# Seven half-size products in place of eight in one feed-forward of a transformer kernel on Trainium2

## The reference

```python
D_MODEL, SEQ, D_FF, FFN_HALF = 1024, 512, 2816, 0.5

def swiglu(h, w13, w2):
    gate, up = jnp.split(h @ w13, 2, axis=-1)
    return (jax.nn.silu(gate) * up) @ w2

# in second_block, layer 0
x = x + jnp.concatenate([y_mix, y_mem], axis=-1) @ w_out[layer]
x = x + FFN_HALF * swiglu(rms_norm(x, norm_g[layer, 2]), ffn_w13[layer, 1], ffn_w2[layer, 1])
```

## Time and profile before

| | |
|---|---|
| median of 3 runs | 2980.66 us (2978.97 to 2982.44) |
| span of the profiled execution | 2978.9 us |
| PE busy | 99%, 13494 matmuls |
| PEld busy | 81% |
| DVE, ACT, POOL busy | 60%, 32%, 8% |
| DMA | 287.55 MB, mean 97 GB/s |

### The profile page before, as it was taken

One profiled execution on the slowest core, in us unless ns is written; L12 is line 12 of the kernel. 1 busy time (PEld: TensorE's weight loads), 2 busy tenths in 40 slices (PEclk: granted clock), 3 DMA queues, 4 the chain that ended last, 5 costly groups with the idle time before them and its releaser, 6 DMA issues.

```text
span 2978.9 us, 36307 instructions
## 1 busy us (share of the span) xinstructions
PE 2962.1 (99%) x13494; PEld 2414.2 (81%) x13494; DVE 1802.2 (60%) x2379; ACT 956.6 (32%) x1292; POOL 224.5 (8%) x105
## 2 busy tenths in 40 slices
PE   9999999999999999999999999999999999999999
PEld 7888788788888888888887888888888886688887
DVE  8897565667766555544467655556555567755542
ACT  4743632333222222222233322222222245332221
POOL 0044330000000000000032000002000021000000
PEclk9999999999999999999999999999999999999999
DMA  4222123223222222223332222232222231122233
GB/s 142 99 92 90 67 92 120 71 96 110 99 94 96 99 95 97 95 95 106 106 121 78 96 99 92 98 106 99 99 99 99 99 113 65 37 98 98 92 106 106
DMA packets 79304, 287.55 MB, mean 97 GB/s; under 512 B 8992, under 2 KB 9248, under 8 KB 78816
## 3 DMA queue, kind: packets, MB, share of 16 engines
q1 hardware_dynamic: 77904, 280.06, 27.9%
q0 software_dynamic: 1296, 6.03, 0.6%
HBM read 283.96 MB, written 2.10 MB: 96 GB/s over the span
## 4 chain that ended last, share of the span: by engine, by line
PE 97%; DVE 2%; ACT 1%; DMA 0%; issue 0%; POOL 0%; SPq 0%; POOLq 0%; ACTq 0%; DVEq 0%
PE ps L667 30%; PE ps L669 30%; PE ps L668 30%; PE ps L1056 1%; PE ps L1292 0%; PE ps L1255 0%; PE ps L831 0%; PE ps L820 0%; PE ps L744 0%; PE ps L1045 0%; PE ps L1258 0%; DVE w_lo L1906 0%; PE ps L806 0%; PE ps L839 0%; PE ps L951 0%
## 5 line engine op out<-in xcount | busy, mean ns | idle before, releaser
L667 PE MATMUL ps<-h_hi,w_hi 128*128 128x512 f32 (+1 forms) x2371 | 928.8, 392 | 3.0 <-DVE w_lo L1906 2.6
L669 PE MATMUL ps<-h_hi,w_lo 128*128 128x512 f32 (+1 forms) x2371 | 919.9, 388 | 0.0
L668 PE MATMUL ps<-h_lo,w_hi 128*128 128x512 f32 (+1 forms) x2371 | 919.6, 388 | 0.0
L1359 ACT ACTIVATE w_hi<-raw 128x1024 fp32r<-128x1024 f32 x524 | 554.0, 1057 | 1008.6 <-DMA raw<-in_wstream 1008.4
L1906 DVE TENSOR_TENSOR w_lo<-raw,w_hi 128x1024 fp32r<-128x1024 f32 x436 | 528.4, 1219 | 134.5 <-ACT w_hi L1359 123.6
L667 PEld LDWEIGHTS ps<-h_hi,w_hi 128*128 128x128 f32 x2371 | 445.6, 188 | 102.5 <-issue 7.7
L668 PEld LDWEIGHTS ps<-h_lo,w_hi 128*128 128x128 f32 x2371 | 445.6, 188 | 92.8 <-issue 3.1
L669 PEld LDWEIGHTS ps<-h_hi,w_lo 128*128 128x128 f32 x2371 | 445.3, 188 | 91.9
L667 PE MATMUL ps<-mid_hi,w_hi 128*128 128x512 f32 x1200 | 468.1, 390 | 0.0
L669 PE MATMUL ps<-mid_hi,w_lo 128*128 128x512 f32 x1200 | 466.9, 389 | 0.0
L668 PE MATMUL ps<-mid_lo,w_hi 128*128 128x512 f32 x1200 | 466.9, 389 | 0.0
(11 more groups left out here) (432 smaller groups left out, 2542.3 us busy)
## 6 DMA issues: line engine op xcount, KB each, us to landing
raw<-in_wstream SPq DMA_DIRECT2D x525, 512.0 KB, 3.2
x<-in_x SPq DMA_DIRECT2D x4, 512.0 KB, 6.3
x_in<-in_x POOLq DMA_DIRECT2D x8, 256.0 KB, 3.0
mem_x<-in_mem POOLq DMA_DIRECT2D x2, 1024.0 KB, 5.3
out<-x SPq DMA_DIRECT2D x8, 256.0 KB, 4.6
tmp<-in_ret_decay POOLq DMA_DIRECT2D x1, 1024.0 KB, 7.4
rope_r<-in_rope_r POOLq DMA_DIRECT2D x1, 512.0 KB, 4.0
mats<-in_mats SPq DMA_DIRECT2D x1, 256.0 KB, 7.9
```

Source lines behind the costliest of these rows:

```text
L667: nc.tensor.matmul(dst, hi_w, hi_x, start=first, stop=False)
L668: nc.tensor.matmul(dst, hi_w, lo_x, start=False, stop=False)
L669: return nc.tensor.matmul(dst, lo_w, hi_x, start=False, stop=last)
L1359: nc.scalar.activation(w_hi[:, n % HL], raw[:, r], ACT.Copy).then_inc(hi_ready, 1)
```

## The change

The product of `s0b_in` is computed in a form of Strassen's scheme (seven products instead of eight, with the sums of Winograd's form). The 1024 channels of x are cut in two halves, its 512 tokens in two halves, and the columns of a unit in gate and up: a 2 x 2 by 2 x 2 block product. A unit is one gate tile and one up tile of 128 columns; there are 22. Each of its seven products has 4 channel tiles x 3 matmuls of 256 columns.

- Weights come from a new tensor `pairs`: 22 units of 128 x 2048 (1 MB), as four blocks of 512 columns: gate and up of the first channel half, gate and up of the second, in the order that the slices of `unit_load` show. The stage `s0b_in` leaves the stream of panels. SP loads two blocks as they are and five more blocks, four of which a DMA then turns into sums: POOL issues `t1 += block`, `t2 += t1`, `t3 += block`, `t4 += t2`, each an accumulating DMA of 256 KB. The loaded block and the sums have two buffers (even and odd units); each load waits for the product of two units before that used the buffer.
- ACT makes the high parts in four slots of `w_hi` that all units share, so each waits for the same product of the unit before. DVE makes the low parts.
- The four sums of blocks of x are made once, by DVE, while `wo0` ends. `wo0` now runs its output tiles in the order 0, 4, 1, 5, ... (`PAIRED`), so that both channel halves of a pair are there. x takes its gain on ACT, squares are made by ACT and added by DVE.
- PE orders the products p1, p2, p4 of the unit before, p5, p6, p3, p7. p1, p6, p7 and p4 add up in one bank, and ACT or DVE takes each state out in between.
- The product of gate and up is kept unsplit; ACT and DVE split the 22 tiles at the end of the units and during the first output tile. The up side isn't multiplied by `rstd` any more; the output of `s0b_out` is (`rooted`).

SP's loads and POOL's sums:

```diff
+            def unit_load(u, i=None):
+                p = u % 2
+                src = A["pairs"][u] if i is None else A["pairs"][bass.ds(i * 2 + u, 1)].rearrange("a p n -> (a p) n")
+                later = i is not None
+                if later:
+                    sp.wait_ge(p2_done, at(u - 1, i, 2))
+                sp.dma_start((pairs_b if p else pairs_a)[:, 0:2], src[:, 0:2 * S].rearrange("p (a n) -> p a n", n=S)).then_inc(b_loaded[p], 16)
+                if later:
+                    sp.wait_ge(p5_done, at(u - 1, i, 2))
+                sp.dma_start(unit_raw("t1", p), src[:, 0:S]).then_inc(t1_loaded[p], 16)
+                if later:
+                    sp.wait_ge(p6_done, at(u - 1, i, 2))
+                sp.dma_start(unit_raw("t2", p), src[:, 3 * S:4 * S]).then_inc(t2_loaded[p], 16)
+                if later:
+                    sp.wait_ge(p3_done, at(u - 1, i, 2))
+                sp.dma_start(unit_raw("c", p), src[:, 3 * S:4 * S]).then_inc(c_loaded[p], 16)
+                if later:
+                    sp.wait_ge(p7_done, at(u - 1, i, 2))
+                sp.dma_start(unit_raw("t3", p), src[:, 2 * S:3 * S]).then_inc(t3_loaded[p], 16)
+                if later:
+                    sp.wait_ge(p4_done, at(u - 1, i, 2))
+                sp.dma_start(unit_raw("t4", p), src[:, S:2 * S]).then_inc(t4_loaded[p], 16)
...
+            unit_load(0)
+            loads(ST["mem0"].n + 4, ST["conv"].n + 3)
+            unit_load(1)
+            loads(ST["conv"].n + 3, ST["s0b_out"].n)
+            with sp.Fori(0, (UNITS - 2) // 2) as i:
+                for u in (2, 3):
+                    unit_load(u, i)
...
+            def unit_sums(u):
+                p = u % 2
+                src = A["pairs"][u]
+                pool.wait_ge(t1_loaded[p], 16 * (u // 2 + 1))
+                pool.dma_start(unit_raw("t1", p), src[:, 2 * S:3 * S], accum_op=ALU.add).then_inc(t1_summed[p], 16)
+                pool.wait_ge(t2_loaded[p], 16 * (u // 2 + 1))
+                pool.wait_ge(t1_summed[p], 16 * (u // 2 + 1))
+                pool.dma_start(unit_raw("t2", p), unit_raw("t1", p), accum_op=ALU.add).then_inc(t2_summed[p], 16)
+                pool.wait_ge(t3_loaded[p], 16 * (u // 2 + 1))
+                pool.dma_start(unit_raw("t3", p), src[:, 3 * S:4 * S], accum_op=ALU.add).then_inc(t3_summed[p], 16)
+                pool.wait_ge(t4_loaded[p], 16 * (u // 2 + 1))
+                pool.wait_ge(t2_summed[p], 16 * (u // 2 + 1))
+                pool.dma_start(unit_raw("t4", p), unit_raw("t2", p), accum_op=ALU.add).then_inc(t4_summed[p], 16)
+            for u in range(UNITS):
+                unit_sums(u)
```

PE's products and their order:

```diff
+            def half_products(kind, x, u, which, first, ks=range(KH)):
+                hi, lo, tile, col0 = X_OF[x]
+                dst, cols = unit_bank(u % 2, which), slice(col0, col0 + H)
+                for k in ks:
+                    sl = slice(P * k, P * k + P)
+                    w1, w0 = unit_high(kind)[:, sl], unit_low(kind, u % 2)[:, sl]
+                    x1, x0 = hi[:, tile + k, cols], lo[:, tile + k, cols]
+                    start = first and k == 0
+                    nc.tensor.matmul(dst, w1, x1, start=start, stop=False, skip_group_check=not first)
+                    nc.tensor.matmul(dst, w1, x0, start=False, stop=False, skip_group_check=not first)
+                    mm = nc.tensor.matmul(dst, w0, x1, start=False, stop=k == KH - 1, skip_group_check=not first)
+                return mm
+            Z1, Z2, Z3 = range(3)
+            def fourth(u, i=None):
+                pe.wait_ge(t4_low, at(u + 1, i, 2))
+                pe.wait_ge(c22_taken, at(u + 1, i, 2))
+                half_products("t4", "a22", u, Z1, False).then_inc(p4_done, 1)
+            def from_sixth(u, i=None, middle=None):
+                pe.wait_ge(t2_low, at(u + 1, i, 2))
+                pe.wait_ge(p1_copied, at(u + 1, i, 2))
+                half_products("t2", "s2", u, Z1, False).then_inc(p6_done, 1)
+                if middle:
+                    middle()
+                pe.wait_ge(c_low, at(u + 1, i, 2))
+                pe.wait_ge(c11_taken, at(u + 1, i, 2))
+                half_products("c", "v4", u, Z3, True).then_inc(p3_done, 1)
+                pe.wait_ge(t3_low, at(u + 1, i, 2))
+                pe.wait_ge(e_taken, at(u + 1, i, 2))
+                half_products("t3", "s3", u, Z1, False).then_inc(p7_done, 1)
+            def unit(u, i=None):
+                pe.wait_ge(b_low, at(u + 1, i, 2))
+                if u >= 2:
+                    pe.wait_ge(c21_taken, at(u - 1, i, 2))
+                else:
+                    pe.wait_ge(drained, ST["wo0"].t + DT)
+                half_products("b11", "a11", u, Z1, True).then_inc(p1_done, 1)
+                if u >= 2:
+                    pe.wait_ge(c12_taken, at(u - 1, i, 2))
+                half_products("b21", "a12", u, Z3, True).then_inc(p2_done, 1)
+                fourth(u - 1, i)
+                pe.wait_ge(t1_low, at(u + 1, i, 2))
+                half_products("t1", "r1", u, Z2, True).then_inc(p5_done, 1)
+                from_sixth(u, i)
+            def first_unit():
+                t = ST["wo0"].t
+                pe.wait_ge(b_low, 1)
+                pe.wait_ge(drained, t + KH + 1)
+                pe.wait_ge(x_low, 4 * KH - 3)
+                half_products("b11", "a11", 0, Z1, True).then_inc(p1_done, 1)
+                pe.wait_ge(drained, t + KH + 2)
+                pe.wait_ge(x_low, 4 * KH - 6)
+                half_products("b21", "a12", 0, Z3, True, range(KH - 1))
+                pe.wait_ge(t1_low, 1)
+                pe.wait_ge(drained, t + KH + 3)
+                pe.wait_ge(x_low, 4 * KH - 5)
+                half_products("t1", "r1", 0, Z2, True, range(KH - 1))
+                pe.wait_ge(x_low, 4 * KH - 2)
+                half_products("b21", "a12", 0, Z3, True, (KH - 1,)).then_inc(p2_done, 1)
+                pe.wait_ge(x_low, 4 * KH - 1)
+                half_products("t1", "r1", 0, Z2, True, (KH - 1,)).then_inc(p5_done, 1)
+                pe.wait_ge(x_low, 4 * KH)
+                from_sixth(0, middle=late_sum)
+            first_unit()
+            unit(1)
+            with pe.Fori(0, 8) as i:
+                for u in (2, 3):
+                    unit(u, i)
+            for u in range(18, UNITS):
+                unit(u)
+            pe.wait_ge(c21_taken, UNITS - 1)
+            gemm("s0b_out", gated_hi, gated_lo, (mid_split, lambda k: k + 1), F2, between=(KH, lambda: fourth(UNITS - 1)))
```

ACT's order of a unit (each `high_` waits for its sum or load and for the product of the unit before):

```diff
+            def high_t1(u, i=None):
+                act.wait_ge(t1_summed[u % 2], at(16 * (u // 2 + 1), i, 16))
+                if u:
+                    act.wait_ge(p5_done, at(u, i, 2))
+                half_high("t1", t1_high, u)
...
+            def unit(u, i=None):
+                high_t3(u, i)
+                first_copied(u, i)
+                high_b(u + 1, i)
+                if u == 1:
+                    act.wait_ge(p4_done, 1)
+                    nc.scalar.activation(tmp[:, 0, right], unit_bank(0, 0), ACT.Copy).then_inc(c21_taken, 1)
+                high_t4(u, i)
+                unit_gate(u - 1, i)
+                fifth_copied(u, i)
+                high_t1(u + 1, i)
+                high_t2(u + 1, i)
+                high_c(u + 1, i)
```

DVE's sums of x, the low parts and the order of a unit:

```diff
+            def low_t1(u, i=None):
+                dve.wait_ge(t2_summed[u % 2], at(16 * (u // 2 + 1), i, 16))
+                half_low("t1", t1_high, t1_low, u, i)
+            def low_t2(u, i=None):
+                dve.wait_ge(t4_summed[u % 2], at(16 * (u // 2 + 1), i, 16))
+                half_low("t2", t2_high, t2_low, u, i)
...
+            def halved_sums(q):
+                k = q // 2
+                dve.wait_ge(z_made, q + 1)
+                if q % 2 == 0:
+                    v.tensor_tensor(tmp[:, 0, right], tmp[:, 0, left], tmp[:, 0, right], ALU.subtract).then_inc(sums_made, 1)
+                    return
+                done(v.scalar_tensor_tensor(out=tmp[:, 2, right], in0=tmp[:, 0, right], scalar=-1.0, in1=tmp[:, 1, right],
+                                            op0=ALU.mult, op1=ALU.subtract))
+                v.tensor_tensor(tmp[:, 2, left], tmp[:, 2, right], tmp[:, 0, left], ALU.add).then_inc(sums_made, 1)
+                v.tensor_tensor(tmp[:, 3, left], tmp[:, 2, right], tmp[:, 1, left], ALU.add).then_inc(sums_made, 1)
...
+            def between_right(u, i=None):
+                p = u % 2
+                dve.wait_ge(p5_copied, at(u + 1, i, 2))
+                dve.wait_ge(p6_done, at(u + 1, i, 2))
+                v.tensor_tensor(stage[:, p, left], stage[:, p, right], unit_bank(p, 0), ALU.subtract).then_inc(e_taken, 1)
+            def second_right(u, i=None):
+                p = u % 2
+                dve.wait_ge(p7_done, at(u + 1, i, 2))
+                v.tensor_tensor(stage[:, p, right], stage[:, p, right], unit_bank(p, 0), ALU.subtract).then_inc(c22_taken, 1)
...
+            def unit(u, i=None):
+                second_right(u - 1, i)
```

(19 more changed lines are left out.)

389 lines of the change are left out of this document (374 added, 15 removed), and 2 rows, old and new, of the table STAGES.

## The result

| | us | |
|---|---|---|
| before | 2981.51 | median of 4 runs, 2978.97 to 2982.44 |
| after | 3075.73 | median of 4 runs, 3068.55 to 3080.16 |
| after / before | 1.032 | 95% interval 1.0307 to 1.0332 |
| predicted | 2988.0 | range 2965 to 3018 |

The change costs 94 us, 3.2%. Slower was the likeliest side, but by 7 us, and the time lies outside the range. The page shows the new thing at once: DMAs have 7% of the chain, where they had 0% before.

The account below looks back on a forecast made before the run. TensorE, busy 99%, was taken to bound the kernel. Stage terms -17.8 + 2.0 + 3.2 + 0.5 + 0.5 = -11.6 us, plus 19 for the DMA loop, gave +7.4 on the median 2980.66: 2988 us, range 2965 to 3018.

Parts of the forecast that it names:

- TensorE's part: In the rewritten stage, 256-column matmuls at 0.1199 us make a unit 10.07 us instead of 10.88: 17.8 us less.
- The mechanism: TensorE idles once per unit, about 0.9 us, until VectorE's subtraction of the seventh product, VectorE held by the fourth sum's DMA.
- The end: In the chain into the next stage, the eighth output tile's extra multiplication costs 0.5 us (0 to 0.7).
- loop one: Closed loop through VectorE's queue, from one fourth product to the next: 6.8 + L, 11.0 us per unit, +19 over 20 units.
- L: Time for one accumulating DMA of 256 KB to land: taken as 4.2 us, ends 3.0 and 5.3.
- loop two: Closed loop on GpSimd's queue, two sums waited for in a row: 2L + 0.58 + 0.54, 10.07 us at L = 4.5.
- The bandwidth estimate: A unit reads 3.93 MB with every add read twice: 9.9 to 10.4 us at the saturated stretches' rates.
- the saturation rival: DMA engines saturate in the new stage: 12.2 us per unit or L above 5, +41 to +43, 3011 us; chance 0.13.
- The rival's sign: In the changed profile, loads landing in 4 us too would show saturation.
- The start: At the stage's start, TensorE waits for the last output-projection tile's sums and splits: 2.0 us (0 to 4).
- My sign for a wrong account of it: A first wait over 5 us in the changed profile would mean the account of the start or engines is wrong.
- the reciprocal: In unit 1, the norm's reciprocal, 3.35 us on VectorE, delays the seventh product's bank: 3.2 us of wait (1 to 5).

Follow-up runs that it names:

- e2_no_adds: The changed kernel without the four accumulating DMAs of every unit, products taken with the blocks as loaded: 2975.98 us, ratio 0.9985 to the kernel before.
- e1_order: The changed kernel with VectorE's subtraction for the fourth product moved ahead of the next unit's lows of t2 and c: 3031.45 us.
- e9_three_sums: e1_order without the sum of t3, whose block is used as loaded: 3032.67 us.
- e7_pool_start: e4_pool_adds with ScalarE's and VectorE's queues reordered at the end of the output projection wo0: 2983.24 us.
- e8_mixed: e1_order's VectorE order and e11_start's start, with t1 and t3 summed by DMA, t2 and t4 by GpSimd's arithmetic: 2976.07 us.
- e11_start: The changed kernel with only ScalarE's and VectorE's queues reordered at the end of wo0, as in e7_pool_start: 3064.25 us.
- e3_copies: The changed kernel with the four accumulating DMAs of a unit made plain copies of the same size, same queue and waits: 3030.92 us.
- e4_pool_adds: The changed kernel with the four sums of a unit made by GpSimd's own arithmetic in place of DMAs: 2991.58 us.
- e6_filled: The changed kernel with 24 more matmuls of 256 columns per unit ahead of the fourth product's wait: 3081.61 us.

## Why the prediction was wrong

**What held.** TensorE's part: 0.12 us per matmul, a unit 10.07 forecast and 10.08 measured where nothing waits. The mechanism: TensorE waits once per unit, for the subtraction of the seventh product, with VectorE held by the fourth sum's DMA. The Trainium skill, Collectives: The Full Stack, section The bandwidth ceiling, says of the reducing step of a ReduceScatter that it is slower because the add needs two source reads, with a measured ratio of 1.93; the trace agrees in size, with a factor of 2.05 in packet time. The end: the step ahead of the next stage's first matmul is 0.93 us too long, 0.21 before, so 0.7 for the forecast 0.5, the upper end of its bounds. The Trainium skill, TensorE: Matmul & The Clock Gate, section Back-to-back issue gap, gives N/2.4 + 2.5 ns for an isolated matmul, by which I estimate 109 ns; the changed kernel's own steps are 120 again.

**The step that failed** is loop one's sum, "6.8 + L" with L = 4.2. The loop was the right one; three of its four terms were too small. Measured on the first unit of the round above, and on average over the 18 units:

| link | forecast | one unit | average |
|---|---|---|---|
| load of t4, to the issue of its sum | 3.1 | 4.6 | 4.7 |
| sum of t4, L | 4.2 | 4.6 | 6.2 |
| two lows, subtraction, to the matmul | 2.1 | 1.8 | 1.8 |
| fourth product, to the load's issue | 1.6 | 3.1 | 2.5 |
| together | 11.0 | 14.0 | 15.2 |

L is the largest part of the miss: 4.6 to 8.9 us, in 9 of 18 units over my upper bound of 5.3. I had added 0.2 us to it for the DMA share, and nothing to the load, while loads of 256 KB land in 3.3 to 3.7 us without the sums (e2_no_adds) and in 4.4 to 6.0 with them (medians by tile). And in 11 units the fourth product runs at the lower clock level, mostly behind a long wait that the loop itself makes.

**The second failed step** is loop two, "10.07 at L = 4.5. It is the later of the two", which I then left out of the sum. By my own terms the other loop is 11.3 at that L, so the sentence was wrong when written. With L = 4.2 for each of its sums loop two would be 9.5; measured, it is 13 us in e1_order where it is what holds TensorE. t2's sum shares its queue and engines with t3's, issued 0.54 us behind. In the changed kernel this cost little, since the queue held t4's sum in two units of 18; it is what was left when loop one was opened, and why that won 2.2 us of a unit's 5.1 and not all.

**The bandwidth estimate** went by bytes at the best rate seen, 9.9 to 10.4. By engine time (0.423 + 0.380 of 250 us, for 16.7 units) a unit needs 12.0 us, the 12.2 that I gave to the saturation rival. But that isn't what set the time: e1_order gained 44 us with every byte in place, and e9_three_sums nothing with 13% fewer. The rival's sign came true as well, loads that land in over 4 us; it doesn't tell full engines from busy ones. The rival had the better number by luck, and 3011 was still 65 us short. But a floor of 12 against the 10.88 of before says that the change could not have won as written.

**The start** was forecast at 2.0 (0 to 4) and is 8.5, plus about 2 us of half clock. My sign for a wrong account of it, a first wait over 5 us, came true. The dependency chain behind the last tile was sound, as the 2.17 of e7_pool_start shows; what I left out is that two engines, each with a fixed order, pass every tile to and fro, 7 us per tile against TensorE's 5.4, so they were late before the chain began. I compared VectorE's busy time with the time there (9.8 of 11 us) and took it as fitting. In return the reciprocal, forecast at 3.2 us of wait, cost nothing in after. With the start mended it showed as 0.83 us in e7_pool_start and 2.92 in e8_mixed, and in e11_start TensorE had no wait there. Start and reciprocal together: 5.2 forecast, 8.5 to 11 measured.

**What stays open**: how much the lower clock of the fourth product adds inside the loop (up to 12 us), how L divides between fixed cost and engine load, and why it is 7.5 us on average in the 8 units that began with a fast fourth product and 5.1 in the other 10.

## What to carry to other kernels

When a change puts DMAs into a closed loop, price every transfer in the loop, loads too, at the load of the new stage, and count engine time per queue (share x span / MB) and not bytes. Then write down each queue's own cycle, the in-order waits of each issuing engine, and compare them: when the longer is opened, the next one sets the pace. Moving one instruction ahead of a wait was worth 44 us here, while making sums on an idle engine was worth 84. Count over many units which of a queue's conditions came last: the one round that I first read in full held one of the two exceptions. Where two engines pass work to each other, the time is the length of that ring; busy shares don't show it.

## What the runs showed of the hardware

- An accumulating DMA takes 2.05 times the engine time of a copy, 97 against 47 us of one engine per MB, in a mixture of which half goes from SBUF to SBUF.
- Its issue takes GpSimd 0.86 to 1.22 us, against 0.54 for the plain copies of e3_copies in the same place and 0.53 to 0.70 before.
- With GpSimd adding beside it, VectorE's tensor_tensor of 512 columns of float32 took up to 1735 ns on average in one place of e4_pool_adds (693 in e2_no_adds), while the lows of 512 columns took 681 to 716. In e8_mixed, with half as many additions, it took 1246, and the lows 791 to 1122 by tile (686 in e2_no_adds).
- In after, when the fourth product started 3.6 to 7.0 us after the start of the matmul before it, TensorE ran it at the lower clock level in 10 of 11 cases, when 1.3 to 3.4 us, in 1 of 8; in e6_filled 2.9 us of waiting behind 3 us of filling did it too.
